# Reordering the last block of a Strassen-Winograd MLP: up and down products in turn, a bank pair of its own, and three partial results added by DMA

## The reference

```
def squared_relu_mlp(h, w1, w2):
    return jnp.square(jax.nn.relu(h @ w1)) @ w2

for i in range(DEPTH):                      # 2
    ...                                     # mixer, attention
    h = rmsnorm(x, norm_ffn_g[i])
    x = x + squared_relu_mlp(h, ffn_w1[i], ffn_w2[i])
return rmsnorm(x, final_norm_g)
```

## Time and profile before

| | us |
|---|---|
| median of 3 runs (1178.56 to 1179.97) | 1178.7 |
| the profiled execution | 1177.56 |
| its span, first to last instruction | 1175.6 |
| PE busy | 1141.2 (97%) |
| DVE busy | 819.1 (70%) |
| ACT busy | 647.2 (55%) |
| POOL busy | 205.1 (17%) |
| mean granted clock of TensorE | 0.988 |

### The profile page before, as it was taken

The page is one execution under the profiler, slowest core; times in us unless marked ns, Lnnn a source line. Parts: engine busy times, 40 slices in busy tenths (PEclk is TensorE's granted clock), DMA queues, the critical chain, the costliest instruction groups (busy, mean ns, idle before and its releaser), DMA issues.

```text
span 1175.6 us, 16200 instructions
## 1 busy us (share of the span) xinstructions
PE 1141.2 (97%) x6556; PEld 1004.3 (85%) x6556; DVE 819.1 (70%) x937; ACT 647.2 (55%) x799; POOL 205.1 (17%) x190
## 2 busy tenths in 40 slices
PE   8999999999999998799999999999999999999887
PEld 7888889999999998688888888888999999999765
DVE  6887646786777776587488655654768677786758
ACT  6764445765665656255444443535676556565535
POOL 0040013112121130112164021001312112012010
PEclk9999999999999999799999999999999999999989
DMA  9532134899888695545232632314589979769453
GB/s 349 203 99 90 46 144 75 219 241 201 188 175 207 146 180 153 99 89 198 89 101 81 215 89 72 106 36 146 95 237 229 207 171 189 199 135 195 106 97 112
DMA packets 48745, 176.59 MB, mean 150 GB/s; under 512 B 5536, under 2 KB 5920, under 8 KB 48032
## 3 DMA queue, kind: packets, MB, share of 16 engines
q0 software_dynamic: 18432, 67.12, 31.6%
q1 hardware_dynamic: 28656, 104.35, 26.6%
q10 hardware_dynamic: 1584, 4.10, 1.0%
HBM read 173.45 MB, written 2.10 MB: 149 GB/s over the span
## 4 chain that ended last, share of the span: by engine, by line
PE 85%; DVE 8%; ACT 3%; issue 2%; DMA 1%; POOL 0%; SPq 0%; ACTq 0%; DVEq 0%; POOLq 0%
PE psum L1947 11%; PE psum L1949 11%; PE psum L1948 11%; PE psum L2227 9%; PE psum L2228 8%; PE psum L2229 8%; PE psum L2207 8%; PE psum L2209 8%; PE psum L2208 8%; DVE w_lo L1225 1%; ACT w_hi L736 1%; DMA w_raw<-in_weights 1%; DVE y_rows L1574 1%; PE psum L2144 1%; PE psum L2266 1%
## 5 line engine op out<-in xcount | busy, mean ns | idle before, releaser
L2227 PE MATMUL psum<-w_lo,slot_hi 128*128 128x512 f32 x448 | 178.9, 399 | 20.5 <-DVE y_rows L1574 20.5
L1225 DVE TENSOR_TENSOR w_lo<-w_sum,w_hi 128x1024 fp32r<-128x1024 f32 x112 | 136.2, 1222 | 87.1 <-ACT w_hi L736 86.9
L736 ACT ACTIVATE w_hi<-w_sum 128x1024 fp32r<-128x1024 f32 x112 | 118.2, 1055 | 113.6 <-PE psum L2229 92.6
L2228 PE MATMUL psum<-w_hi,slot_hi 128*128 128x512 f32 x448 | 177.7, 397 | 0.0
L2229 PE MATMUL psum<-w_hi,slot_lo 128*128 128x512 f32 x448 | 177.0, 395 | 0.0
L2207 PE MATMUL psum<-xs_s_lo,w_hi 128*128 128x256 f32 x512 | 145.3, 284 | 0.0
L2209 PE MATMUL psum<-xs_s_hi,w_lo 128*128 128x256 f32 x512 | 144.9, 283 | 0.0
L2208 PE MATMUL psum<-xs_s_hi,w_hi 128*128 128x256 f32 x512 | 144.9, 283 | 0.0
L1225 DVE TENSOR_TENSOR w_lo<-w_raw,w_hi 128x1024 fp32r<-128x1024 f32 x80 | 97.6, 1222 | 43.5 <-ACT w_hi L736 43.3
L1897 POOL DMA_DIRECT2D w_sum<-in_down x64 | 55.4, 866 | 393.2 <-DVE w_lo L1225 393.2
L736 ACT ACTIVATE w_hi<-w_raw 128x1024 fp32r<-128x1024 f32 x80 | 83.8, 1054 | 71.5 <-PE psum L2209 52.2
(11 more groups left out here) (229 smaller groups left out, 2656.5 us busy)
## 6 DMA issues: line engine op xcount, KB each, us to landing
w_raw<-in_weights SPq DMA_DIRECT2D x89, 512.0 KB, 3.7
w_sum<-in_down POOLq DMA_DIRECT2D x64, 512.0 KB, 6.9
w_sum<-in_down SPq DMA_DIRECT2D x48, 512.0 KB, 4.7
w_raw<-in_up POOLq DMA_DIRECT2D x48, 512.0 KB, 7.0
w_raw<-in_up SPq DMA_DIRECT2D x32, 512.0 KB, 3.8
up<-in_up SPq DMA_DIRECT2D x16, 512.0 KB, 4.5
up<-in_up POOLq DMA_DIRECT2D x16, 512.0 KB, 7.2
x<-in_x_t SPq DMA_DIRECT2D x2, 1024.0 KB, 8.4
```

The costliest lines, as they stand in the source:

```text
L736: act.activation(w_hi[:, c % RING, :], buffer(kind, i), ACT.Copy).then_inc(whi_ready, 1)
L1225: dve.tensor_tensor(w_lo[:, c % RING, :], buffer(kind, SUM_BUFFER[STAGE[p][0]] + half), w_hi[:, c % RING, :].bitcast(F32), ALU.subtract).t ...
L2227: pe.matmul(to, s_hi[:, k, tok], w_lo[:, c % RING, cols], start=first, stop=False, skip_group_check=True)
L2228: pe.matmul(to, s_hi[:, k, tok], w_hi[:, c % RING, cols], start=False, stop=False, skip_group_check=True)
```

## The change

Order of steps: in the last two blocks up and down alternate to the end, so up P7, down P7, up P4, down P4. Block 3's down products then run P2 (first half), P1, P5, P3, P6, P2 (second half), P7, P4.

Banks: in block 3 the chain P1, P6, P7, P4 accumulates in banks 2 and 3 (`PAIR_A`) in place of banks 0 and 1, which keep block 2's result. The transposes behind layer 0's MLP and the gate's first bank uses exchange banks 0, 1 and 2, 3 to fit.

Results: three of them (block 2's P4, block 3's P1 and P5) are not read by DVE. ACT copies each with its row scale into an SBUF tile (`stage`, two instructions of 128 x 512), and POOL issues a DMA that adds the tile to `y_rows` (`add_staged`). PE waits for the ACT copy (`staged_ready`) where it waited for DVE's read. Later DVE reads of the same quarter wait for the DMA (`rows_added`).

Sums: s2 of the last block goes to its own tile (`last_s2`), s4 is computed from it, and s3 last. The slots of block 3's operands are dealt anew: P2 has slot 0, P5, P6, P4 slot 1, P1, P3, P7 slot 2. ACT and DVE prepare P5's operand first, then P1's.

At the start of each MLP the first four bank-wide transposes move behind up P3's first half.

```diff
-LAST_DOWN = (("P1", 0), ("P1", 1), ("P2", 0), ("P5", 0), ("P5", 1), ("P3", 0), ("P3", 1), ("P6", 0), ("P6", 1),
+LAST_DOWN = (("P2", 0), ("P1", 0), ("P1", 1), ("P5", 0), ("P5", 1), ("P3", 0), ("P3", 1), ("P6", 0), ("P6", 1),
              ("P2", 1), ("P7", 0), ("P7", 1), ("P4", 0), ("P4", 1))
-            ("U", "P6"), ("D", "P6"), ("U", "P7"), ("U", "P4"), ("D", "P7"), ("D", "P4"))
+            ("U", "P6"), ("D", "P6"), ("U", "P7"), ("D", "P7"), ("U", "P4"), ("D", "P4"))
+STAGED = ((FB - 2, "P4"), (FB - 1, "P1"), (FB - 1, "P5"))
-LAST_SLOTS = {"P1": 0, "P2": 1, "P5": 2, "P3": 0, "P6": 2, "P7": 0, "P4": 2}
+LAST_SLOTS = {"P2": 0, "P5": 1, "P1": 2, "P3": 2, "P6": 1, "P7": 2, "P4": 1}
-    return PAIR_E if (b, p) == (FB - 1, "P2") else ROWS_PAIR[p]
+    if b < FB - 1:
+        return ROWS_PAIR[p]
+    return {PAIR_X: PAIR_A, PAIR_Y: PAIR_E if p == "P2" else PAIR_Y}[ROWS_PAIR[p]]
...
+                def stage(i):
+                    b, p = STAGED[i]
+                    scale = negative_r2 if p == "P5" else r2
+                    for t in range(2):
+                        if p == "P5" and t == 0:
+                            act.wait_ge(tile_ready, 2 * l + 1)
+                        else:
+                            act.wait_ge(psum_ready, N.ready[f"f{l}", "D", b, p, 1] + 1)
+                        row = 2 * ROWS_PART[p][0] + t
+                        act.activation(staged[i][:, t, :], psum[:, rows_pair(b, p) + t, :], ACT.Copy,
+                                       scale=scale[:, row:row + 1]).then_inc(staged_ready, 1)
...
                 ahead("U", c, "P7", 0)
-                operand(c, "P1", a11, h=0)
+                operand(c, "P2", a12, h=1)
+                ahead("U", c, "P7", 1)
+                squared(c, 2, a22, "P7")
+                ahead("D", b, "P7", 0)
+                ahead("D", b, "P7", 1)
+                ahead("U", c, "P4", 0)
+                ahead("U", c, "P4", 1)
+                ahead("D", b, "P4", 0)
+                last_quarter(c)
+                ahead("D", b, "P4", 1)
+                operand(c, "P5", s1, summed=1)
+                operand(c, "P1", a11, h=0)
...
                 b = FB - 1
+                ahead("D", b, "P2", 0)
+                stage(0)
                 ahead("D", b, "P1", 0)
+                ahead("D", b, "P1", 1)
+                operand(b, "P3", a12, summed=3)
+                ahead("D", b, "P5", 0)
                 if l:
                     act.dma_start(last_gain[:], last_gain_d.partition_broadcast(P)).then_inc(gain_loaded, 16)
+                stage(1)
                 ahead("D", b, "P5", 1)
-                operand(b, "P6", a11, summed=3)
+                stage(2)
+                operand(b, "P6", last_s2, summed=2)
...
                 ahead("U", c, "P7", 0)
                 read(b, "P6")
+                operand(c, "P2", a12)
+                ahead("U", c, "P7", 1)
+                c22(c)
+                ahead("D", b, "P7", 0)
+                ahead("D", b, "P7", 1)
+                ahead("U", c, "P4", 0)
+                read(b, "P7")
+                ahead("U", c, "P4", 1)
+                ahead("D", b, "P4", 0)
+                sum_s1(c)
+                ahead("D", b, "P4", 1)
+                last_sum_s2(c)
+                operand(c, "P5", s1)
                 operand(c, "P1", a11)
...
+            def add_staged(l, i):
+                b, p = STAGED[i]
+                part = ROWS_PART[p]
+                pool.wait_ge(rows_read, read_count(l, FB - 2, {"P4": "P7", "P1": "P2", "P5": "P7"}[p]))
+                if p == "P4":
+                    pool.wait_ge(rows_read, read_count(l, FB - 3, "P4"))
+                pool.wait_ge(staged_ready, 2 * (3 * l + i) + 2)
+                pool.dma_start(y_part(*part), staged[i][:], accum_op=ALU.add).then_inc(rows_added, 16)
...
                         add_quarters(l, "D", b, p)
                         if b < FB - 1:
                             add_quarters(l, "U", b + 1, p)
+                        elif p != "P6":
+                            add_staged(l, ("P1", "P5", "P3").index(p))
...
                 sum_done(0, "P2")
-                rows_from_tiles(0)
                 wait_split((f"xs{l}", "P3"))
                 pe.wait_ge(kept_half, l + 1)
                 up(0, "P3", 0)
+                rows_from_tiles(0)
...
                 down_product(b, "P6")
                 sum_done(c, "P6")
                 up_product(c, "P7")
-                pe.wait_ge(sum_half, 3 * l + 3)
-                up(c, "P4", 0)
-                sum_done(c, "P7")
-                up(c, "P4", 1)
                 read_done(b, "P6")
                 down_product(b, "P7")
+                sum_done(c, "P7")
+                up_product(c, "P4")
                 read_done(b, "P7")
                 down_product(b, "P4")
                 b = FB - 1
-                read_done(b - 1, "P4")
-                down_product(b, "P1", fresh=True)
                 kept_done(b, "P3")
                 down(b, "P2", 0, fresh=True).then_inc(psum_ready, 1)
+                kept_done(b, "P4")
+                down_product(b, "P1", fresh=True)
                 read_done(b - 1, "P3")
                 down_product(b, "P5", fresh=True)
-                waits = [read_count(l, b, "P5", t) for t in range(2)]
-                down(b, "P3", 0, tile_waits=waits).then_inc(psum_ready, 1)
+                waits = [6 * l + 4 + t + 1 for t in range(2)]
+                down(b, "P3", 0, tile_waits=waits, waited=staged_ready).then_inc(psum_ready, 1)
                 down(b, "P3", 1).then_inc(psum_ready, 1)
-                read_done(b, "P1")
+                pe.wait_ge(staged_ready, 6 * l + 4)
                 down_product(b, "P6")
```

More of the change, by code:

```diff
@@ L304, in mlp_order @@
         for j, step in enumerate(MLP_STEPS):
-            if step == ("U", 0, "P3", 0):
+            if step == ("U", 0, "P3", 1):
                 for n in range(4):
@@ L330, in mlp_order @@
             for m in range(4, 8):
-                self.add(("xt", m), "bank", at=(6, 7, 2, 3)[m - 4])
+                self.add(("xt", m), "bank", at=(6, 7, 0, 1)[m - 4])
             for m in GATE_ORDER:
@@ L425, in trunk_kernel @@
     xs_s3 = at(z_off, "xs_s3", [P, 4, NMEM])
+    last_s2 = at(z_off, "last_s2", [P, 4, NMEM])
+    staged = [at(a_off + 16 * KB + 4 * KB * i, f"staged_{i}", [P, 2, 512]) for i in range(3)]
     edge_lo = at(region(GROUPS * PAD * 4), "edge_lo", [P, GROUPS, PAD], F32R)
@@ L597, in read_count, with added_count @@
     def read_count(l, b, p, t=1):
-        order = LAST_READS if b == FB - 1 else READS
-        return 14 * (FB * l + b) + 2 * order.index(p) + t + 1
+        before = sum(2 * len(READS[a]) for a in range(b)) + l * sum(2 * len(order) for order in READS.values())
+        return before + 2 * READS[b].index(p) + t + 1
+    def added_count(l, i):
+        return 16 * (3 * l + i + 1)
     TOK = (slice(0, NMEM), slice(NMEM, S))
@@ L1535, in sum_s1, with last_sum_s2, last_sum_s4 @@
                     dve.tensor_tensor(s1[:], a22[:], a21[:], ALU.subtract).then_inc(s_step, 1)
+                def last_sum_s2(b):
+                    dve.wait_ge(s_step, s_count(l, b, 1))
+                    dve.wait_ge(sum_ready, sum_count(l, b, "P6"))
+                    dve.scalar_tensor_tensor(out=last_s2[:], in0=s1[:], scalar=-1.0, in1=a11[:], op0=ALU.mult,
+                                             op1=ALU.subtract).then_inc(s_step, 1)
+                def last_sum_s4(b):
+                    part_done(b, "P2")
+                    dve.wait_ge(s_step, s_count(l, b, 2))
+                    dve.scalar_tensor_tensor(out=a12[:], in0=a12[:], scalar=-1.0, in1=last_s2[:], op0=ALU.mult,
+                                             op1=ALU.subtract).then_inc(s_step, 1)
                 def sum_s3(b):
@@ L1760, in last_sum @@
                 def last_sum(t, ready):
+                    if t == 2:
+                        dve.wait_ge(rows_added, added_count(1, 0))
                     dve.wait_ge(psum_ready, ready + 1)
-                    dve.scalar_tensor_tensor(out=y_rows[:, t, COLS[0]], in0=psum[:, PAIR_X + t - 2, :], scalar=r2[:, t:t + 1],
+                    dve.scalar_tensor_tensor(out=y_rows[:, t, COLS[0]], in0=psum[:, PAIR_A + t - 2, :], scalar=r2[:, t:t + 1],
                                              in1=y_rows[:, t, COLS[0]], op0=ALU.mult, op1=ALU.add).then_inc(lasty_ready, 1)
@@ L2374, in mlp @@
                     read_done(b, "P7")
-                    kept_done(b, "P4")
+                    pe.wait_ge(staged_ready, 2)
                     tiles_from_rows(4)
```

74 lines of the change are left out of this document (25 added, 49 removed).

## The result

| | before | after |
|---|---|---|
| median | 1178.63 us of 4 runs | 1161.51 us of 4 runs (1160.81 to 1161.55) |
| ratio | | 0.9852, 95% interval 0.9835 to 0.9869 |
| the profiled execution | 1177.56 | 1160.81 |
| its span | 1175.6 | 1159.0 |
| mean granted clock | 0.988 | 0.998 |

A forecast was written before the change was run, and what follows sets the result against it. PE, busy 97%, bounds the kernel, so only its idle or slow time can be won: 28.9 less 2.3, 1.1, 3.6, 1.5 and 0.5 is 19.9, giving 1158.8 us (1156 to 1163); 8 in 10: 1153 to 1168.

The forecast's parts named there:

- slow clock: PE in the MLP tail: 0.5 us lost to the lower clock behind the longest new wait.
- Parts 1: Down P4 of block 2 and down P1 of block 3: the four old waits go, minus 28.9 us.
- 2: Down P1 of block 3: waits 1.15 us per layer for its operand, last in DVE's queue; plus 2.3.
- 5: Start of each MLP: transposes no longer cover ScalarE's half copy of P5; 0.74 us per layer, plus 1.5.
- Part 4: Down P4 of block 3: three more adds, 2.7 us each, delay its weights; 3.1 in layer 1, 0.5 in layer 0.
- (a): Staged adds cheap, 1.4 us of data or less; P3 and P4 losses vanish: 1154.1 us, chance 0.16.
- (b): Staged adds cost 1.3 to 1.9 times as much, at P3 and P4: up to 1177 us, chance 0.11.
- (c): Slower than before: staged adds at some 5.3 us of data or more, losses at P3 and P4; chance 0.05.
- (e): Change misses its aim: read of P7 or P1's slot still holds PE, half lost, 1172 us; chance 0.04.
- Part 3: Down P3 of block 3: ScalarE's copy of P5 waits behind an add; 0.2 us layer 1, 0.9 layer 0.
- E: End of up P4 of block 3, the zero from which tail times are counted; 1109.0 in layer 1.
- rival (d): Short PE waits of 1 to 3 us already bring the 1.2 GHz level: 1167 us, chance 0.06.

The follow-up runs named there:

- experiment 3: Kernel after, with ScalarE and DVE preparing P1's operand ahead of P5's: ratio 0.9864 to the kernel before, 1163.91 us.
- experiment 4: Kernel after, with the first four bank-wide transposes back ahead of up P3's first half: ratio 0.9832 to the kernel before, 1159.88 us.
- Experiment 1: Kernel after, with ScalarE's copy of P5's result ahead of the w_hi of P6's first half: ratio 0.9841 to the kernel before, 1162.19 us.
- Experiment 5: Kernel after, with the next layer's first four weight loads started behind the last P4 w_lo of block 3: ratio 0.9859, 1161.62 us.
- experiments 9: Kernel after without staging: DVE reads the three results, P5's read ahead of P1's read and sum s3: ratio 0.9781, 1153.58 us.
- 7: Kernel after without its six staged adds, ScalarE's copies kept, output lacking three results per layer: ratio 0.9782 to the kernel before, 1152.41 us.
- experiment 2: Kernel after, with each staged add issued one product later, behind the next weight adds: ratio 0.9809 to the kernel before, 1156.96 us.
- 10: Kernel after with DVE reads for staging, P5's read first, P1's operand first, transposes back ahead of up P3: ratio 0.976, 1151.15 us.
- experiment 8: Kernel after, with the three additions per layer made by GpSimd itself, issued behind the next weight adds: ratio 0.9817, 1156.8 us.

## Why the prediction was nearly right, point by point

| step | predicted, us | in the profile after |
|---|---|---|
| four waits and their slow clock | 28.9 gone | gone |
| start of the MLP, both layers | 1.5 | 1.7 (2.65 less 0.94) |
| P1, both layers | 2.3 | 2.1 |
| P3, layer 0 | 0.9 | 3.95 |
| P3, layer 1 | 0.2 | 1.0 |
| P7, layer 1 | 0 | 1.1 |
| P4, layer 1 | 3.1 | 1.7 |
| P4, layer 0 | 0.5 | 0 |
| slow clock | 0.5 | 1.7 |
| new losses | 9.0 | 13.2 |

28.9 less 13.2 is 15.7; the spans differ by 16.6, so 0.9 us is not assigned. The total came nearer than its terms: P3, P7 and the slow clock cost 6.2 us more than forecast, the start and P1 together as forecast, and P4 1.9 less. The sum had not foreseen that the one would lower the other, so a part of its closeness is luck.

**Parts 1, 2 and 5 held.** No wait of the old kind is left. P1's 1.15 came as 0.96 and 1.10 for the low part of P1's operand, and experiment 3 removed it by nothing but the order of the operands. The start came as the work on `kept_p` that the transposes had covered, and experiment 4 brought it back to 0.47.

**Part 4 had the right price and the wrong place.** A staged add is 3.0 us of 16 engines by the queues' rows, or 3.2, against 2.7 taken, so rivals (a), (b) and (c), of 1.4 or less and of 3.5 and more, are all out; so is (e), since no old wait is left. Layer 1 loses 3.8 us behind P1 against 3.3 predicted. But the sum charged all of it to P4, the last place: a row of adds that falls steadily behind shows first where PE first meets it. What P3 (1.0) and P7 (1.1) waited moved P4's due time back, and P4's own wait came out smaller. P7 was not foreseen; the step that I left out is the read of P6 behind the `w_lo` that waits for an add. Experiment 1 shows the shift in the open: moving the copy took P3's two waits away, 5.0 us, and P6, P7 and P4 together waited 4.5 us more than before it.

**Part 3 is the term that was mis-sized,** in layer 0: 0.9 us between bounds of 0 and 2.2, measured 3.95, outside both. Two of its figures were too small. I took P1's add to land 0.7 us later than the 5.4 of an undisturbed one, since the weight loads start earlier in the new order; it took 7.8, almost the 8.2 of before, so the loads had not got out of its way: 1.7 more. And P5's add, 6.8 from issue by the sum, took 7.8: 1.0 more. Experiment 5 confirms the first of them: with the loads moved P1's add takes 5.5 and P3's wait falls by 2.35.

The sum also has a sign wrong. Its steps put the copy at E+20.0 and P3 at E+20.2, which is a cover of 0.2 us, and it was booked as a wait; by its own steps P3 would wait 0.5 in layer 0 and nothing in layer 1, and the upper bound would be 2.6, not 2.2. With E at 466.44, the start of down P4, POOL issued P1's add 0.5 us and P5's another 0.2 us behind the reckoning; 0.5, 1.7, 1.0 and 0.7 are 3.9, against 3.95. In layer 1 (E at 1101.72) P1's add took 5.7, near its 5.4; P5's was issued 0.6 behind its E+11.6 and took 7.7 for 6.8, and P3 waits 1.0.

**The slow clock** was set at 0.5 us and cost 1.7, because P3 waited 3.95. Of rival (d) a part is true after all, from 2.36 us on (below); waits of 1 to 2 us, which the forecast had, kept 1.00.

**The Trainium skill** (DMA: Bandwidth & Descriptors, "Anatomy of one DMA — SWDGE (gpsimd) path") gives 3.2 us as an estimate for such a transfer by itself. No add of the kernels before and after landed in less than 5.2, and in the tail of the kernel after it was 5.4 to 13.9; by the page Parts 3 and 4 would have been nothing, and with the slow clock they are 9.5 of the 13.2 us lost.

**Where the gain went.** The reordering is worth what experiments 9 and 7 show, 0.978, or 26 us of the 28.9. The staged adds give back 8 of it, 5 of which come back when they are only issued later (experiment 2); the order of P1's and P5's operands and the transposes leave some 2.5 more to win (9 against 10). The staged adds free DVE of six reads, yet with the reads in the right order DVE had room for them at no cost that can be measured (9 against 7). The resource that was full was the queue of adding DMAs, at 91.4% of 16 engines over 28 us of layer 1's tail and 101% in six of them, against 62.9% without the staged adds.

## What to carry to other kernels

Before moving work from an engine to DMAs, look at the DMA queue in the stage in question, not over the span: 33.6% there was 101% for six microseconds here, and a transfer that nobody waits for still delays the one behind it that somebody waits for. When several consumers hang on one slow row, clearing the first wait moves it to the next; the size of the loss is read from the row, its places are not. If a queue is in order, put first what is waited for: that alone was worth 5 us, and keeping the three reads on DVE, in the right order, 8.

## What the runs showed of the hardware

- An adding DMA of 512 KB took 2.9 us of all 16 engines from DRAM and 3.0 to 3.2 from SBUF, by the shares above, and landed after 5.4 us alone (the first staged one of each layer too) and up to 13.9 behind others. Issuing the staged one kept GpSimd busy 1.21 us, a weight add 0.86.
- The granted clock went to about 0.50 behind waits of PE of 2.36, 2.38, 2.40, 2.56, 2.84 and 3.60 to 5.53 us, and stayed at 1.00 behind all those looked at of up to 2.07 (2.07, 2.03, 1.81, 1.69, 1.62). Behind 2.40 the first matmul was still fast (0.50 us) and the slow level came after it; behind 2.38, in experiment 4, the first was already slow (0.77 us). Experiment 1, windows of 503:505 and 505:507:

```profile
503.00:505.00 2.00, 1.19 (x5) 1.00 (x6) 1.89 (x3) 0.00 (x0) 0.00 (x0) 0.98 1.09 217
505.00:507.00 2.00, 2.00 (x7) 1.52 (x6) 0.57 (x1) 1.06 (x1) 0.00 (x0) 0.50 0.86 168
```

- An addition on GpSimd of 128 x 1024 took 2.73 us and stretched a DVE subtraction beside it from 1.22 to 3.62, which ended 1.08 us after GpSimd's did; in all six such pairs of experiment 8 it was 1.08 to 1.09, whenever DVE had started. DVE's reads, with one of their two inputs in PSUM, kept their 1.40 for two beside it. The Trainium skill (SBUF — State Buffer, "Who interferes with whom") says that a DVE instruction with two SBUF inputs contends with a GpSimd instruction that reads SBUF, and that the ports which the two share are an exclusive lock. The trace agrees: 483.10 + 2.73 plus one undisturbed 1.22 is 487.05, against 486.91.
- ScalarE's copy with a row scale from PSUM to SBUF, 128 x 512, took 0.67 us against the 0.58 of the plain one in the earlier trace rows.
